# Row parts of the residual itself in half tiles, one norm factor per slot, and the last two tiles routed one by one

## The reference

```python
h = rmsnorm(x, norm_mix_g)
x = x + hybrid_mixer(h, ...)      # neighbourhood attention and gated linear attention, then w_out
h = rmsnorm(x, norm_ffn_g)
x = x + hierarchical_moe(h, ...)
return rmsnorm(x, final_norm_g)

def hierarchical_moe(x, ...):
    g_sel = argmax(x @ w_grp + b_grp)                     # 1 of 4 groups
    top_v, top_i = top_k(exp_logits of that group, 2)     # 2 of 8 experts in it
    for e in range(32):
        y = y + combine[:, e] * ((silu(x @ w_gate[e]) * (x @ w_up[e])) @ w_down[e])
```

## Time and profile before

| what | value |
|---|---|
| median of 3 runs | 795.13 us (795.09 to 797.71) |
| the profiled execution's own time | 796.33 us |
| its span | 794.5 us |
| TensorE busy | 738.7 us (93%) |
| VectorE, ScalarE, GpSimd busy | 225.8, 146.2, 97.4 us |
| moved by DMA | 234.76 MB |
| mean granted clock of TensorE | 0.984 |

### The profile page before, as it was taken

The page is one execution under the profiler, slowest core; times in us unless marked ns, Lnnn a source line. Parts: engine busy times, 40 slices in busy tenths (PEclk is TensorE's granted clock), DMA queues, the critical chain, the costliest instruction groups (busy, mean ns, idle before and its releaser), DMA issues.

```text
span 794.5 us, 13652 instructions
## 1 busy us (share of the span) xinstructions
PE 738.7 (93%) x6164; PEld 374.9 (47%) x6164; DVE 225.8 (28%) x437; ACT 146.2 (18%) x304; POOL 97.4 (12%) x82
## 2 busy tenths in 40 slices
PE   5999999999999997999999999999999989988960
PEld 3444454464455466455545455544545454434410
DVE  3008782005566167211111111111111111111126
ACT  5152330024345264000000000000000000000004
POOL 0442340000000055000000000000000000000002
PEclk9999999999999999999999999999999999999995
DMA  9430230401550648899999999999999999999965
GB/s 332 109 106 14 93 107 1 159 9 54 196 227 2 252 171 318 320 412 422 428 424 422 426 425 423 422 428 423 424 425 425 422 422 418 421 420 421 414 276 205
DMA packets 36971, 234.76 MB, mean 295 GB/s; under 512 B 5922, under 2 KB 7330, under 8 KB 19120
## 3 DMA queue, kind: packets, MB, share of 16 engines
q1 hardware_dynamic: 34352, 229.66, 71.0%
q0 software_dynamic: 2560, 4.20, 1.4%
HBM read 227.55 MB, written 10.49 MB: 300 GB/s over the span
## 4 chain that ended last, share of the span: by engine, by line
PE 73%; DMA 18%; DVE 3%; SPq 3%; ACT 2%; issue 1%; DVEq 0%; POOLq 0%
PE bank L484 21%; PE bank L785 18%; DMA arena<-in_w_up 16%; PE bank L808 9%; PE bank L765 8%; PE bank L652 4%; PE bank L696 3%; SPq L416 1%; PE bank L613 1%; PE bank L685 1%; SPq L417 1%; PE bank L670 1%; PE bank L787 1%; PE bank L797 1%; PE bank L788 1%
## 5 line engine op out<-in xcount | busy, mean ns | idle before, releaser
L785 PE MATMUL bank<-arena 128*64 128x512 f32 x928 | 205.3, 593 | 11.5 <-DMA arena<-in_w_up 10.6
L484 PE MATMUL bank<-arena 128*128 128x512 f32 x384 | 167.0, 594 | 0.0
L785 PEld LDWEIGHTS bank<-arena 128*64 128x64 f32 x928 | 67.9, 137 | 144.6 <-issue 134.4
L1112 DVE TENSOR_TENSOR arena<-bank,arena 128x512 f32<-128x512 f32 (+1 forms) x96 | 47.8, 512 | 304.1 <-ACT arena L1071 212.4
L808 PE MATMUL bank<-arena 128*64 128x512 f32 x512 | 116.9, 598 | 0.5 <-ACT arena L1075 0.5
L484 PEld LDWEIGHTS bank<-arena 128*128 128x128 f32 x384 | 72.3, 190 | 89.8 <-issue 89.5
L765 PEld LDWEIGHTS bank<-arena 128*128 128x128 bf16 x3072 | 97.4, 99 | 24.8 <-issue 23.9
L765 PE MATMUL bank<-arena 128*128 128x64 bf16 x3072 | 101.7, 194 | 0.3 <-DVE arena L1112 0.3
L1568 POOL DMA_INDIRECT y_tok<-arena x32 | 31.3, 978 | 431.0 <-DVE arena L1428 402.4
L1071 ACT ACTIVATE arena<-bank 128x256 f32<-128x256 f32 x32 | 12.3, 384 | 355.1 <-PE bank L785 320.1
L808 PEld LDWEIGHTS bank<-arena 128*64 128x64 f32 x512 | 33.9, 136 | 57.1 <-issue 54.5
(11 more groups left out here) (160 smaller groups left out, 483.8 us busy)
## 6 DMA issues: line engine op xcount, KB each, us to landing
arena<-in_w_down SPq DMA_DIRECT2D x31, 2048.0 KB, 30.1
arena<-in_w_gate SPq DMA_DIRECT2D x25, 2048.0 KB, 23.6
arena<-in_w_up SPq DMA_DIRECT2D x24, 2048.0 KB, 22.4
arena<-in_w_up SPq DMA_DIRECT2D x14, 1024.0 KB, 28.6
arena<-in_w_in SPq DMA_DIRECT2D x6, 2048.0 KB, 8.0
arena<-in_w_gate SPq DMA_DIRECT2D x12, 1024.0 KB, 27.8
arena<-y_tok SPq DMA_DIRECT2D x8, 512.0 KB, 5.5
arena<-in_x SPq DMA_DIRECT2D x4, 512.0 KB, 6.9
```

Source lines behind the costliest of these rows:

```text
L484: m = pe.matmul(pbank[unit_bank(n)][:], lhs(k), rhs(k), start=(k == 0), stop=(k == KC - 1))
L785: mm = pe.matmul(both, xT[:, k], gate_and_up(e, k, cols), start=(k == 0), stop=(k == KC - 1))
L1112: return nc.vector.tensor_tensor(out_, a, b, op)
```

## The change

The row parts are made of x1 itself, without the norm factor, half a tile at a time: `hi` is a plain cast, `rest` a subtraction (VectorE alone), and GpSimd keeps only the last remainder. x1 is read by chunks of 128 neighbouring columns; for that the host reorders gate and up weights, so that partition p of chunk k holds row 128 k + p. The norm factor is applied later, for each slot of an expert: `split_rstd` splits `rstd2` in three bfloat16 parts, `destinations()` carries them to the slots with 160 columns for 64, and `silu` and `hidden` multiply by `rstd_slot`. Tiles 2 and 3 are routed one by one, a cast and two small operations leave the routing chain, router(2) is issued in two pieces, and there are 5 and 2 keep_clock matmuls for 12 and 3.

```diff
-        wg_d = w_gate.rearrange("l e (p k) f -> (l e) p k f", k=KC)
-        wu_d = w_up.rearrange("l e (p k) f -> (l e) p k f", k=KC)
+        wg_d = w_gate.rearrange("e p (k f) -> e p k f", k=KC)
+        wu_d = w_up.rearrange("e p (k f) -> e p k f", k=KC)
...
         def x1_by_chunk(t):
-            return x1[:, t].rearrange("p (q k) -> p k q", k=KC)
+            return x1[:, t].rearrange("p (k q) -> p k q", k=KC)
...
-                    pe.wait_ge(first_picked, 1 if t1 <= 2 else 2)
+                    pe.wait_ge(first_picked, max(t1 - 1, 1))
...
-                            mm = pe.matmul(pbank[7][64 * half:64 * half + 64, 0:2 * EXPERTS], by_slot[k][:, t],
+                            mm = pe.matmul(pbank[7][64 * half:64 * half + 64, 0:5 * EXPERTS], by_slot[k][:, t],
...
             ranks(0, 2)
-            router(2)
+            router(2, range(0, KC // 2))
             x1_T(3)
+            router(2, range(KC // 2, KC))
+            router(3)
             pick_rows(0, 0, 1)
-            router(3)
+            ranks(2, 3)
             pick_rows(0, 1, 2)
-            keep_clock(12)
-            ranks(2, TT + 1)
-            keep_clock(3)
-            pick_rows(0, 2, TT)
+            keep_clock(5)
+            ranks(3, 4)
+            pick_rows(0, 2, 3)
+            keep_clock(2)
+            pick_rows(0, 3, 4)
+            ranks(TT, TT + 1)
             for e in range(EXPERTS):
                 gate_up(e)
+                if e == 0:
+                    destinations()
                 if e < LAST:
                     pick_rows(e + 1, 0, TT - 1)
-                if e == 0:
-                    destinations()
                 hidden_T(e)
...
-            def square(t):
-                act.wait_ge(x1_done, 2 * (t + 1))
-                nc.scalar.activation(junk2[t], x1[:, t], ACT.Square, accum_out=ssq2[:, t:t + 1]).then_inc(sumsq_done, 1)
+            def square(t, half):
+                act.wait_ge(x1_done, 2 * t + half + 1)
+                act.wait_ge(sumsq_done, TT + 2 * t + half)
+                nc.scalar.activation(junk2, x1[:, t, half * 512:(half + 1) * 512], ACT.Square, scale=D ** -0.5,
+                                     accum_out=ssq2[:, t, half:half + 1]).then_inc(sumsq_done, 1)
...
-            def hi(t, ks):
-                act.wait_ge(sumsq_done, TT + t + 1)
-                act.wait_ge(rstd_done, TT + t + 1)
-                nc.scalar.activation(h2_part[t][0][:, ks], x1_by_chunk(t)[:, ks], ACT.Identity,
-                                     scale=rstd2[:, t:t + 1]).then_inc(hi_done, 1)
-
-            def mid(t, ks, rest_sem, rests):
-                act.wait_ge(rest_sem, rests)
-                nc.scalar.copy(h2_part[t][1][:, ks], rest2[t % 2][:, ks]).then_inc(mid_done, 1)
-
-            square(0)
+            def hi(t, half):
+                act.wait_ge(x1_done, 2 * t + half + 1)
+                nc.scalar.copy(h2_part[t][0][:, halves[half]], x1_by_chunk(t)[:, halves[half]]).then_inc(hi_done, 1)
+
+            def mid(t, half):
+                act.wait_ge(rest_done, 2 * t + half + 1)
+                nc.scalar.copy(h2_part[t][1][:, halves[half]], rest2[t % 2][:, halves[half]]).then_inc(mid_done, 1)
+
+            hi(0, 0)
+            square(0, 0)
...
+            hi(3, 0)
+            square(3, 0)
+            mid(3, 0)
+            hi(3, 1)
+            square(3, 1)
+            mid(3, 1)
+            x1_T_evict(3)
             square_root(3)
-            x1_T_evict(3)
-            hi(3, halves[0])
-            hi(3, halves[1])
-            mid(3, halves[0], rest_done, 3)
-            mid(3, halves[1], rest_pool, 2)
...
             def silu(e):
                 act.wait_ge(gu_done, e + 1)
-                nc.scalar.activation(hid[e % RING], pbank[e % RING][:, 0:256], ACT.Silu).then_inc(sil_done, 1)
+                if e == 0:
+                    act.wait_ge(rows_joined, 1)
+                nc.scalar.activation(hid[e % RING], pbank[e % RING][:, 0:256], ACT.Silu,
+                                     scale=rstd_slot[:, e:e + 1]).then_inc(sil_done, 1)
...
-                then(nc.vector.tensor_copy(gidx[:, ts], itop8[:, ts, 0:1]))
-                for t in range(t0, t1):
-                    m = nc.vector.tensor_scalar(gout[:, t], iota[:, 0:GROUPS], gidx[:, t], LOWEST, ALU.not_equal, ALU.mult)
-                then(m)
...
+                then(tt(gout[:, ts], iota[:, 0:GROUPS].unsqueeze(1).broadcast_to((P, n, GROUPS)),
+                        itop8[:, ts, 0:1].broadcast_to((P, n, GROUPS)), ALU.not_equal))
                 for t in range(t0, t1):
-                    m = tt(lg_in[:, t].rearrange("p (g e) -> p g e", g=GROUPS), lg[:, t, 8:].rearrange("p (g e) -> p g e", g=GROUPS),
-                           gout[:, t].unsqueeze(2).broadcast_to((P, GROUPS, PER_GROUP)), ALU.add)
+                    m = nc.vector.scalar_tensor_tensor(lg_in[:, t].rearrange("p (g e) -> p g e", g=GROUPS),
+                                                       gout[:, t].unsqueeze(2).broadcast_to((P, GROUPS, PER_GROUP)), LOWEST,
+                                                       lg[:, t, 8:].rearrange("p (g e) -> p g e", g=GROUPS), ALU.mult, ALU.add)
...
-                then(nc.vector.tensor_copy(eid[:, ts], eidx[:, ts, 0:2]))
...
-                dve.wait_ge(rank_mm_done, 1 if t0 == 0 else 2)
+                dve.wait_ge(rank_mm_done, max(t1 - 1, 1))
+                incl = pbank[2 if t1 < TT else 1][:, 0:TT * EXPERTS].rearrange("p (t e) -> p t e", e=EXPERTS)
...
+            def split_rstd():
+
+                tt(gexp, lg[:, :, 0:GROUPS], gtop[:, :, 0:1].broadcast_to((P, TT, GROUPS)), ALU.subtract).then_inc(cdiff_done, 1)
+                tt(ediff, etop[:, :, 1:2], etop[:, :, 0:1], ALU.subtract).then_inc(cdiff_done, 1)
+                then(nc.vector.tensor_copy(rstd_part[0], rstd2))
+                then(tt(rstd_rest[0], rstd2, rstd_part[0], ALU.subtract))
+                then(nc.vector.tensor_copy(rstd_part[1], rstd_rest[0]))
+                then(tt(rstd_rest[1], rstd_rest[0], rstd_part[1], ALU.subtract))
+                then(nc.vector.tensor_copy(rstd_part[2], rstd_rest[1]))
+                then(nc.vector.tensor_copy(eid, eidx[:, :, 0:2]))
...
-            def rest(t, ks, his):
-                dve.wait_ge(rstd_done, TT + t + 1)
-                dve.wait_ge(hi_done, his)
+            def rest(t, half):
+                dve.wait_ge(hi_done, 2 * t + half + 1)
                 if t >= 2:
-                    dve.wait_ge(parts_done, t - 1)
-                nc.vector.scalar_tensor_tensor(rest2[t % 2][:, ks], x1_by_chunk(t)[:, ks], rstd2[:, t:t + 1],
-                                               h2_part[t][0][:, ks], ALU.mult, ALU.subtract).then_inc(rest_done, 1)
+                    dve.wait_ge(parts_done, 2 * (t - 2) + half + 1)
+                tt(rest2[t % 2][:, halves[half]], x1_by_chunk(t)[:, halves[half]], h2_part[t][0][:, halves[half]],
+                   ALU.subtract).then_inc(rest_done, 1)
 
             residual(0, 0)
+            rest(0, 0)
             residual(0, 1)
+            rest(0, 1)
+            residual(1, 0)
             mean_square(0)
+            rest(1, 0)
             inverse_root(0)
-            residual(1, 0)
             residual(1, 1)
             x1_T_evict(0)
+            rest(1, 1)
             mean_square(1)
+            residual(2, 0)
+            rest(2, 0)
             inverse_root(1)
-            rest(0, all_k, 1)
             x1_T_evict(1)
-            residual(2, 0)
             residual(2, 1)
+            rest(2, 1)
             route_groups(0, 2)
             mean_square(2)
-            inverse_root(2)
             route_experts(0, 2)
             residual(3, 0)
             x1_T_evict(2)
-            rest(2, all_k, 3)
+            rest(3, 0)
+            inverse_root(2)
             residual(3, 1)
             first_slots(0, 2)
+            rest(3, 1)
+            x1_T_evict(3)
             mean_square(3)
-            x1_T_evict(3)
+            route_groups(2, 3)
             inverse_root(3)
-            rest(3, halves[0], 4)
-            route_groups(2, 4)
-            route_experts(2, 4)
-            first_slots(2, 4)
+            route_experts(2, 3)
+            route_groups(3, 4)
+            route_experts(3, 4)
+            first_slots(2, 3)
+            first_slots(3, 4)
+            split_rstd()
...
-                    then(tt(prod, hot[k], incl, ALU.mult))
+                    then(tt(prod, hot[k], code, ALU.mult))
...
+                    for i in range(3):
+                        tt(by_expert[k][:, :, 2 + i], hot[k], rstd_part[i].unsqueeze(2).broadcast_to((P, TT, EXPERTS)), ALU.mult)
...
+                dve.wait_ge(rank_mm_done, 4)
+                nc.vector.tensor_reduce(most, pbank[1][:, TT * EXPERTS:(TT + 1) * EXPERTS], AX.X, ALU.max).then_inc(most_done, 1)
...
-                tt(hid[e % RING], pbank[e % RING][:, 256:512], hid[e % RING], ALU.mult).then_inc(hid_done, 1)
```

(24 more changed lines are left out.)

114 lines of the change are left out of this document (58 added, 56 removed).

## The result

| what | before | changed |
|---|---|---|
| median of the runs made side by side | 796.26 us (795.09 to 797.78, 6 runs) | 789.97 us (789.52 to 792.21, 6 runs) |
| profiled execution, its span | 796.33, 794.5 us | 789.99, 788.2 us |
| VectorE, GpSimd busy | 225.8, 97.4 us | 226.4, 85.5 us |

The ratio is 0.9926, with a 95% interval from 0.9907 to 0.9945: faster by 0.7%. The forecast was 789.9 us, counted from a median before of 795.13 us; the one measured beside the changed kernel is 796.26 us.

The account below looks back on a forecast made before the run. The start of gate_up(0), waiting for routing, was taken to set when weight transfers fill the queue, and so the end. −5.9 and +0.65 sum to −5.25 us: median 795.13 to 789.9 us, range 787.2 to 794.6.

Parts of the forecast that it names:

- fixed point: End of the last output projection, 298.04 us: nothing TensorE issues ahead of it is changed, so it should not move.
- The stage, 5.9 us: From the last projection to gate_up(0): the residual and routing chain shortens, so gate_up(0) starts 5.9 us earlier, at about 309.65.
- one tile's routing: VectorE's routing of tile 2 or 3 alone: 2.4 us, with 3.5 as the ceiling and 1.65 as the floor.
- The loss in expert 0: After gate_up(0): destinations(), with 160 columns for 64, stands ahead of pick_rows(1) and costs 0.65 us more.
- Nothing later gives it back or adds to it: After gate_up(1): the −5.25 us reach the end whole, since loads keep the same shapes and bytes.
- the hole at 336 us stays: Shallow gap in the transfers at 336 to 338 us (324 GB/s): it remains, being set by TensorE's pace.
- the hole at 316 us: Transfer gap at 316 to 320 us before the change: closed by the earlier half of up(3), with 1 us of margin.
- A granted clock of 1.00 throughout: Sign for the changed profile: gate_up(0) at 309.6 with TensorE's clock never falling; a fall before it means wrong.
- rival 1: Routing tiles 2 and 3: pair-like cost or GpSimd block, 1 to 2.2 us later, clock could fall; 791.6 to 793.6 us; chance 0.17.
- Rival 2: Routing: one tile costs only 1.65 us, so the gain is 6 to 7 us, 788.1 to 789.1 us; chance 0.06.
- Rival 3: Weight queue: a transfer, not TensorE, sets when it fills, so no gain; 794 to 796 us; chance 0.07.
- Rival 4: Late weight loads: the new memory order lowers the rate; 1.3% cancels the gain, 2.3% give 799.2 us; chance 0.06.

Follow-up runs that it names:

- e1: The changed kernel with tiles 2 and 3 routed together as a pair again; median 791.07 us, ratio 0.9932 to 0.9963 against the kernel before.
- e6: The changed kernel with one half of gate(3) loaded early, right behind gate(2); median 789.83 us, ratio 0.9901 to 0.9930 against the kernel before.
- e2: The changed kernel with 24 more keep_clock matmuls ahead of gate_up(0); median 794.3 us, ratio 0.9975 to 0.9994 against the kernel before.
- e7: The changed kernel with destinations() issued behind the picks of expert 1, as before the change; median 791.02 us, ratio 0.9917 to 0.9949 against the kernel before.
- e9: The changed kernel once more, unchanged, for a second profile; median 790.42 us, ratio 0.9920 to 0.9950 against the kernel before.
- e11: The kernel before once more, unchanged, for a second profile; 796.52 us (one run).

## Why the prediction was right, and where it was not

**The bound.** The end followed the start of gate_up(0): the medians above stand in the order of up(4), but for breaches of up to 1.3 us (e1 with +33.61 and 791.07 beside e6 with +33.75 and 789.83). Delaying gate_up(0) alone (e2) took back two thirds or more of the gain at the end (3.9 of 5.1 or 4.3 of 6.3 us). So the forecast's mechanism held: −5.25 us were predicted, the medians moved by 6.3 us the first time and by 5.1 the second (795.49 to 790.42). That the first median, 789.97, lies so near 789.9 is in part luck: the median before was 1.13 us higher than the one the forecast started from, and the gain 1 us larger. From up(2) to the start of the last gate_up, where the scatter of the last part doesn't count, the gain is 5.30 us in the first profile (457.64 to 452.34) and 5.05 in the second (452.59).

**The fixed point.** "298.04 is my fixed point": in the changed kernel the projection ends at 296.96. This is not the change. The kernel before, run again, issues up(2) at 296.82, 1.25 us sooner than in its first profile. A profile's own offset belongs in the range.

**The stage, 5.9 us.** It gained 6.65 with the clock at 1.00 and 5.17 when it fell (17.52 − 12.35). The stage was shortened where the forecast had it, by VectorE coming free earlier; of its terms, from the end of the projection: router(3) over at +5.36 predicted, +5.27 measured; `rest` 0.66, measured 0.69; one tile's routing 2.4, measured 2.2 (from `both_b` of tile 2, over at 302.24, to that of tile 3, over at 304.48), so `both_b` of tile 3 at +8.06 predicted, +7.52 measured. With that the picks of tile 3 ended at +10.0, 0.8 us sooner than laid out, and nearly all of it reached gate_up(0).

**The loss in expert 0, 0.65 us.** Wrong in size: 0.06 (17.52 + 21.29 became 10.87 + 21.35). The 16 matmuls with 160 columns take 0.72 us, not 1.1, for 0.44: scaling by columns was the wrong rule here. The list ahead of rows_split fitted under gate_up(0), as predicted (312.2 against 314.8). e7 shows what the new place of destinations() is worth, 1.83 us at up(4).

**"Nothing later gives it back or adds to it", "the hole at 336 us stays".** The hole did not stay: in the 3 us behind the issue of up(4) the transfers now move 380 GB/s for 275 (348 in e9, 295 in e11). With the shorter stage and the hole at 316 us nearly closed, more is left in the queue there, 0.56 MB (0.35 in e9) against 0.04 before (0.20 in e11). Whether anything was given back differs by profile. In the first, 6.59 us at up(4) became 5.30 at the last gate_up, so 1.29 were lost; in e9, 5.11 became 5.05, as forecast. That the first profile's sum comes out is thus luck in part: the stage and expert 0 gave 1.34 us more than forecast, and nearly as much went again. Why they went in this profile and not in e9 is open; that the backlog took them is only argued.

**"A granted clock of 1.00 throughout".** True for one profile of two; a fall ahead of gate_up(0) was on the prediction's own list of signs of being wrong. The fall that rival 1 priced is there in e9, with 1.48 us, in spite of TensorE's short gaps. The forecast came out in e9 even so because the stage was 0.75 us quicker and the loss in expert 0 was 0.6 us smaller than it said, which together make up for nearly all of the fall.

**The rivals.** Rival 1's block by GpSimd occurred, small: `tt` over 128x4 at 300.55 took 0.41 us where its like takes 0.16, and ended with GpSimd's subtraction (299.79 + 1.16). Another, `mean_square` on VectorE at 290.58, took 0.84 for 0.15 and ended at 291.42 with a GpSimd subtraction begun at 290.25:

```profile
290.25 1.15 POOL L1595 TENSOR_TENSOR arena<-arena 128x512 bf16<-128x512 f32 x1 [4.89 <-ACT arena L1051]
290.58 0.84 DVE L1359 SCALAR_TENSOR_TENSOR arena<-arena 128x1 f32<-128x1 f32 x1
```

By the Trainium skill (SBUF — State Buffer, section Who interferes with whom) such a pair shuts each other out; the two rows agree. The eight `rest` did not meet a subtraction: mean 690 ns in the groups by form. Rival 2 came half true: up(4) came 6.59 us sooner in the first profile, as it had it, though not because a tile's routing cost its floor of 1.65 us. Rival 3, that transfers set the end, is refuted as the main mechanism, since the end moves with TensorE's stage, most plainly in e2. Rival 4 is refuted: 425 against 424 GB/s. (Its price was a little off: 2.3% of 415 us on 789.9 give 799.4 us, not 799.2.)

## What to carry to other kernels

Delay the step that is said to set the end, by a known amount: if the end follows, as in e2, the bound is found. Matmuls issued only to hold the clock must not stand ahead of work that somebody waits for; when the clock falls all the same, they lengthen the path (1.48 us here, 0.32 without them). Take a second profile of both kernels before a term near 1 us is read from a pair of them, and measure to the last step that the change can reach rather than to the end: here the scatter behind it was as large as the term. When part of a change seems to give the same in both directions, look whether the clock fell in the same place.

## What was not expected of the hardware

- The granted clock fell in one execution and not in another of the same program, with no wait of TensorE behind the last projection but one of 0.6 us that ended at 299.75. In each of the seven profiles with a fall, it was at 0.50 for about 3.4 us (e9: the windows of one us from 302 to 306 have 0.61, 0.50, 0.50 and 0.69).
- Two executions of the same kernel differ by up to 1.25 us in when they reach the last projection, and by up to 1.6 us in what lies behind up(4); in the kernel before, nearly all of it lies behind the start of the last gate_up, where neither profile waits for weights.
- A matmul group of 16 grew from 0.44 to 0.72 us when its columns grew from 64 to 160.
